# Forget-gate attention: gate bias and causal mask added by VectorE, probabilities turned through HBM by GpSimd's queue

## The chip, the cores and the metric

One core of a Trainium2 chip runs the whole program. The metric is the device time in microseconds of one execution; the kernel before took 1055.29 us (median of 3 runs, 1054.19 to 1055.32).

## What is computed

Two transformer blocks in a row on one sequence of 256 tokens with 1024 channels, all in float32. The change concerns one part of the second block, the attention with a forget gate ("fox"), of 8 heads with 128 channels each:

```python
def fox_attention(q, k, v, f_logit):
    """q,k,v: (B,S,H,dh); f_logit: (B,S,H). logit[t,s] = q.k/sqrt(dh) + sum_{s<j<=t} log f_j, s<=t."""
    c = jnp.cumsum(jax.nn.log_sigmoid(f_logit.astype(jnp.float32)), axis=1).transpose(0, 2, 1)
    ...
        s = jnp.einsum('bqhd,bkhd->bhqk', qi, k32) * scale
        s = s + ci[..., None] - c[:, :, None, :]
        s = jnp.where(kpos[None, :] <= qpos[:, None], s, -jnp.inf)
        p = jax.nn.softmax(s, axis=-1)
        return jnp.einsum('bhqk,bkhd->bqhd', p, v32)
```

The term c of the query is the same for a whole row of scores, so softmax drops it; what is left is a bias by key and the causal mask. The rest of the second block is a gated linear recurrence in chunks ("hgrn2"), a memory attention and two gated feed-forward parts.

## The kernel before

**Weights.** They come as units of 128x2048 floats. SyncE loads them into one of 6 slots (`load`, L591 to L608, two DMAs at L603); for unit u it first waits until TensorE is through with unit u - 6 (L598). ScalarE copies each to a rounded float32r tile `high` (L1368), VectorE subtracts to get the remainder `rest` (L1964), and TensorE multiplies three times, high x high, high x rest and rest x high (`unit`, L820 to L822), 24 matmuls of 512 columns per unit.

**The order of the work.** The projection of the second block, `win2`, has 18 column blocks, thus 36 units. Each engine's program has a loop `for u in range(36)` with a fixed place for every piece of other work: HG_SLOT for the recurrence's levels, FOX_SLOT for the attention: TensorE computes the scores of head n after unit 26 + n and the output of head n - 3 behind them (`fox(n)`, L1173). After the loop comes the block `brA`, in the middle of whose first half stands the last head's output.

**The gates.** In step 7 VectorE cumulates the logarithms of the gates in `fcum`, 40 rows by 256 tokens, where rows 0 to 7 and 32 to 39 hold the same 8 heads (L2522 to L2529). In step 8 ScalarE rounds them to `fbias` (L1742), and VectorE makes rows 32 to 39 the remainder (L2606); the rest of `fbias` is zero (L2531). `fbias` has 384 columns: the 128 keys of the first query tile, then the 256 keys of the second. `fcum` lies in the place into which ScalarE drains the recurrence's inputs in step 9 (`hi_`).

**One head.** `fox(n)` on TensorE: a matmul with a column of `identr`, broadcast, spreads head n's bias over the partitions (L1176, float32r, 384 columns); a matmul of a bf16 identity with `causal` adds the mask on the two diagonal tiles (L1178, 256 columns); two float32 score matmuls add q.k (L1181, recorded as 4). VectorE takes the negated maximum of each query tile (L2553), ScalarE exponentiates with it as the bias and sums (L1814), VectorE scales by the reciprocal of the sum (`fox_scale`, L2081, with L2086 and L2090) and turns the blocks of 32x32 (L2092) into one of 3 slots of `fpT`. SyncE stores that to HBM and reads it back by 4 DMAs in the transposed order of blocks (`turn_probabilities`, L656). These stand behind the weight loads in `load(u)`: the store of head h in unit 32 + h of `win2`, the read one unit later. TensorE multiplies with the values (L1189, L1190), VectorE copies the result out (L2634, L2648).

**GpSimd** runs the differences of the recurrence's decays (`diff`, L751; `cross_diff`, L740), which end near 607 us, and loads gains and small constants by its own queue (L803). After the differences it waits for the last head's output and then loads the memory (L801).

## Time and profile before

| | us |
|---|---|
| median of 3 runs | 1055.29 |
| profiled execution | 1056.9 |
| its span | 1055.1 |
| TensorE busy | 1044.2 (99%) |
| VectorE busy | 755.5 (72%) |
| ScalarE busy | 598.6 (57%) |
| GpSimd busy | 71.0 (7%) |

The profiled execution took 1.8 us more than its span, from the first to the last instruction, and 1.6 us more than the median. Busy times count instructions at work; matmuls are pipelined, so their durations overlap, and the distance between the starts of two is what one costs. TensorE's granted clock is at the full level throughout (0.999 on average).

### The profile page before, as it was taken

Reading aid. Unit: us, or ns where it says so; the run is one execution under the profiler, and the core shown is the slowest. Engines: PE = TensorE matmul, PEld = TensorE weight load, DVE = VectorE, ACT = ScalarE, POOL = GpSimd, SP = SyncE. Lnnn points to the kernel's source line nnn. Section 1 sums busy time; section 2 is a strip of 40 time slices with the busy share of each in tenths; the row PEclk is TensorE's granted clock in tenths of the full one; section 3 lists DMA queues with packets and bytes.
Section 4 is the critical chain, followed back from the end, with each engine's and each line's share of the span. In section 5 each row is a group of like instructions: output and inputs, shape, how many; then the busy total and the mean of one; then the engine's idle time right before and its main releaser. Section 6 shows DMA issues by size and latency. Waiting matters only on the chain.

```text
span 1055.1 us, 12945 instructions
## 1 busy us (share of the span) xinstructions
PE 1044.2 (99%) x4939; PEld 871.8 (83%) x4939; DVE 755.5 (72%) x901; ACT 598.6 (57%) x800; POOL 71.0 (7%) x59
## 2 busy tenths in 40 slices
PE   9999999999999999999999999999999999999997
PEld 7888888878888888888888888888879988888886
DVE  5768777776787676468997778868778666867642
ACT  6473767665384645448774645554366657565531
POOL 1200000000000000000434600000000000000000
PEclk9999999999999999999999999999999999999999
DMA  9945889896487787558857855889875346878751
GB/s 364 390 137 173 293 256 306 272 302 212 177 278 241 246 229 233 188 201 271 250 171 222 240 162 179 266 264 324 298 263 183 120 164 208 236 241 237 246 163 40
DMA packets 97645, 243.89 MB, mean 231 GB/s; under 512 B 15104, under 2 KB 41904, under 8 KB 97456
## 3 DMA queue, kind: packets, MB, share of 16 engines
q1 hardware_dynamic: 94016, 231.51, 67.6%
q0 software_dynamic: 3136, 11.23, 3.1%
q8 instruction: 39, 0.64, 0.2%
q10 hardware_dynamic: 432, 0.33, 0.1%
q14 instruction: 22, 0.18, 0.0%
HBM read 220.48 MB, written 22.54 MB: 230 GB/s over the span
## 4 chain that ended last, share of the span: by engine, by line
PE 76%; DMA 9%; DVE 7%; SPq 3%; issue 2%; ACT 2%; DVEq 0%; ACTq 0%
PE ps L820 17%; PE ps L822 17%; PE ps L821 17%; DMA gv_turned<-gv_blocked 5%; PE ps L857 5%; PE ps L859 5%; PE ps L858 5%; DVE rest L1964 2%; PE ps L954 1%; SPq L641 1%; DMA y_turned<-y_blocked 1%; PE ps L1144 1%; PE ps L1253 1%; PE ps L1255 1%; PE ps L1254 1%
## 5 line engine op out<-in xcount | busy, mean ns | idle before, releaser
L1964 DVE TENSOR_TENSOR rest<-raw,high 128x2048 fp32r<-128x2048 f32 x129 | 295.4, 2306 | 74.7 <-ACT high L1368 74.0
L820 PE MATMUL ps<-high,xt_high 128*128 128x512 f32 x824 | 324.6, 394 | 0.2 <-DVE rest L1964 0.2
L821 PE MATMUL ps<-rest,xt_high 128*128 128x512 f32 x824 | 321.0, 390 | 0.0
L822 PE MATMUL ps<-high,xt_rest 128*128 128x512 f32 x824 | 321.0, 390 | 0.0
L1368 ACT ACTIVATE high<-raw 128x2048 fp32r<-128x2048 f32 x129 | 244.3, 1910 | 68.6 <-DMA raw<-in_units_dram 68.5
L822 PEld LDWEIGHTS ps<-high,xt_rest 128*128 128x128 f32 x824 | 154.7, 188 | 32.3
L820 PEld LDWEIGHTS ps<-high,xt_high 128*128 128x128 f32 x824 | 154.9, 188 | 31.9 <-DVE rest L1964 0.6
L821 PEld LDWEIGHTS ps<-rest,xt_high 128*128 128x128 f32 x824 | 154.9, 188 | 30.9
L1969 DVE SCALAR_TENSOR_TENSOR rest<-raw,wgain,high 128x512 fp32r<-128x512 f32 x176 | 119.1, 746 | 35.7 <-ACT high L1372 35.7
L1372 ACT ACTIVATE high<-raw,wgain 128x512 fp32r<-128x512 f32 x176 | 110.9, 716 | 9.5 <-DMA raw<-in_units_dram 9.5
L1628 ACT ACTIVATE act<-ps,recips 128x256 f32<-128x256 f32 x44 | 18.4, 470 | 85.1 <-PE ps L822 85.0
L821 PE MATMUL ps<-rest,ht_high 128*128 128x512 f32 x168 | 65.4, 389 | 0.0
L822 PE MATMUL ps<-high,ht_rest 128*128 128x512 f32 x168 | 65.4, 389 | 0.0
L820 PE MATMUL ps<-high,ht_high 128*128 128x512 f32 x168 | 65.4, 389 | 0.0
L857 PE MATMUL ps<-high,xt_high 128*128 128x512 f32 x152 | 60.6, 399 | 1.3 <-DVE rest L1964 1.3
L859 PE MATMUL ps<-high,xt_rest 128*128 128x512 f32 x152 | 59.4, 391 | 0.0
L858 PE MATMUL ps<-rest,xt_high 128*128 128x512 f32 x152 | 59.2, 390 | 0.0
L1388 ACT ACTIVATE xt_high<-ps 128x512 fp32r<-128x512 f32 x26 | 15.2, 598 | 58.4 <-PE ps L954 53.0
L2313 DVE SCALAR_TENSOR_TENSOR hid<-ps,recips,act 128x256 f32<-128x256 f32 x44 | 19.2, 478 | 39.7 <-ACT act L1628 39.6
L821 PEld LDWEIGHTS ps<-rest,ht_high 128*128 128x128 f32 x168 | 31.5, 188 | 6.6
L820 PEld LDWEIGHTS ps<-high,ht_high 128*128 128x128 f32 x168 | 31.6, 188 | 6.5
L822 PEld LDWEIGHTS ps<-high,ht_rest 128*128 128x128 f32 x168 | 31.5, 188 | 6.5
(372 smaller groups left out, 1446.0 us busy)
## 6 DMA issues: line engine op xcount, KB each, us to landing
raw<-in_units_dram SPq DMA_DIRECT2D x350, 512.0 KB, 5.0
gv_turned<-gv_blocked SPq DMA_DIRECT2D x11, 512.0 KB, 7.9
gv_t<-gv_turned SPq DMA_DIRECT2D x44, 128.0 KB, 3.1
turned<-blocked SPq DMA_DIRECT2D x22, 256.0 KB, 5.3
hid_t<-turned SPq DMA_DIRECT2D x88, 64.0 KB, 4.1
fox_turned<-fqT SPq DMA_DIRECT2D x6, 512.0 KB, 3.3
raw<-in_units_dram SPq DMA_DIRECT2D x8, 256.0 KB, 4.4
fqT<-fox_turned SPq DMA_DIRECT2D x16, 128.0 KB, 4.2
```

What stands on the lines that cost most here:

```text
L820: pe.matmul(out, sh, wh, start=first, stop=False)
L821: pe.matmul(out, sh, wr, start=False, stop=False)
L822: mm = pe.matmul(out, sr, wh, start=False, stop=last)
L857: pe.matmul(out, sh, wh, start=first, stop=False)
L858: pe.matmul(out, sh, wr, start=False, stop=False)
L859: mm = pe.matmul(out, sr, wh, start=False, stop=last)
L1368: act.activation(high[:, u % SLOTS, c], raw[:, u % SLOTS, c], ACT.Copy).then_inc(unit_high, 1)
L1372: ins = act.activation(high[:, u % SLOTS, c], raw[:, u % SLOTS, c], ACT.Copy, scale=g[:, k:k + 1])
L1628: act.activation(act_[:, j % 2, tt, :], gate_values[:, tt, :], ACT.Silu, scale=recips[:, c:c + 1])\
L1964: vec.tensor_tensor(rest[:, slot, c], raw[:, slot, c], high[:, slot, c].bitcast(F32), ALU.subtract).then_inc(unit_rest, 1)
L1969: ins = vec.scalar_tensor_tensor(rest[:, slot, c], raw[:, slot, c], g[:, q:q + 1], high[:, slot, c].bitcast(F32), ALU.mult, ALU.subtract)
L2313: ins = vec.scalar_tensor_tensor(hid[:, j % 2, :, tt, :], fold(values[:, tt, :]), recips[:, c + tt:c + tt + 1], fold(act_[:, j % 2, tt, :] ...
```

## The change

GpSimd prepares the bias. SyncE stores `fcum` to HBM once (`store_biases`, after the load of unit 13 of `win2`). For each head GpSimd reads the head's row back, spread over the 128 partitions, into one of three float32 tiles (`spread_bias`), and adds `causal` on the two diagonal tiles (`mask_bias`). TensorE computes the score products alone. VectorE's instruction for the maximum becomes one that reads scores and bias, writes -(scores + bias) over the scores in PSUM and keeps the minimum, which is the negated maximum; ScalarE's exponential has the scale -1. Store and reads of the probabilities go from SyncE's queue to GpSimd's. GpSimd's order is: spread 0, spread 1, mask 0, mask 1, then for each head h: spread h + 2, store h, mask h + 2, read h (4 DMAs).

The diff, cut:

```diff
-        fbias = place("fbias", [P, P + S], F32R, area + 62 * KB)
+        fbias = [place(f"fbias{n}", [P, P + S], F32, area + k * KB) for n, k in enumerate((62, 28, 54))]
...
+        fcum_dram = nc.dram_tensor("fcum_rows", (HH, P + S), F32, kind="Internal").ap()
+        def bias_home(h):
+            return fbias[0 if h % 2 == 0 else 1 + h // HALF]
...
-            def turn_probabilities(u):
-
-                h = u - UNIT["win2"] - 33
-                if 0 <= h < HH:
-                    sync.wait_ge(fp_stored, 16 * (h + 1))
-                    src = fp_turned[h].rearrange("(q i) (r e) -> r i q e", q=4, r=4)
-                    for r in range(4):
-                        sync.dma_start(fpT[32 * r:32 * r + 32, h % 3, :].rearrange("p (q e) -> p q e", q=4), src[r]).then_inc(fp_landed[h % 3], 16)
-                h += 1
-                if 0 <= h < HH:
-                    sync.wait_ge(fp_blocked, h + 1)
-                    sync.dma_start(fp_turned[h], fpT[:, h % 3, :]).then_inc(fp_stored, 16)
+            def store_biases(u):
+
+                if u == UNIT["win2"] + 13:
+                    sync.wait_ge(sem("fcum_ready"), 1)
+                    for c0, w in ((0, P), (P, S)):
+                        sync.dma_start(fcum_dram[:, c0:c0 + w], fcum[0:HH, 0:w]).then_inc(fcum_stored, 16)
...
+            def spread_bias(h):
+
+                if h == 1:
+                    pool.wait_ge(aux_done, AUX["lv", 1, 128, 0][0] + 1)
+                elif h == HALF + 1:
+                    pool.wait_ge(aux_done, AUX["fs", HALF - 1][0] + 1)
+                elif h:
+                    pool.wait_ge(sem("fox_max"), TT * (h - 1))
+                pool.dma_start(bias_home(h)[:, :], fcum_dram[h].partition_broadcast(P)).then_inc(fbias_landed[h % 2], 16)
+
+            def mask_bias(h):
+
+                pool.wait_ge(fbias_landed[h % 2], 16 * (h // 2 + 1))
+                d = bias_home(h)[:, :].rearrange("p (n c) -> p n c", n=3)[:, 0:3:2, :]
+                pool.tensor_tensor(d, d, causal[:, :, :], ALU.add).then_inc(fbias_masked, 1)
+
+            def store_probabilities(h):
+
+                pool.wait_ge(fp_blocked, h + 1)
+                pool.dma_start(fp_turned[h], fpT[:, h % 3, :]).then_inc(fp_stored, 16)
+
+            def read_probabilities(h):
+
+                pool.wait_ge(fp_stored, 16 * (h + 1))
+                src = fp_turned[h].rearrange("(q i) (r e) -> r i q e", q=4, r=4)
+                for r in range(4):
+                    pool.dma_start(fpT[32 * r:32 * r + 32, h % 3, :].rearrange("p (q e) -> p q e", q=4), src[r]).then_inc(fp_landed[h % 3], 16)
...
+                    pool.wait_ge(fcum_stored, 32)
+                    pool.wait_ge(consts1_landed, 16 * CONSTS1)
+                    for h in range(2):
+                        spread_bias(h)
+                    for h in range(2):
+                        mask_bias(h)
+                    for h in range(HH):
+                        if h + 2 < HH:
+                            spread_bias(h + 2)
+                        store_probabilities(h)
+                        if h + 2 < HH:
+                            mask_bias(h + 2)
+                        read_probabilities(h)
...
-                    pe.matmul(out[:, 0:P + S], identr[:, n:n + 1].to_broadcast([P, P]), fbias[:, :], start=True, stop=False)
-                    diagonal = out[:, 0:P + S].rearrange("p (n c) -> p n c", n=3)[:, 0:3:2, :]
-                    pe.matmul(diagonal, identb[:, :], causal[:, :, :], start=False, stop=False)
...
-                        mm = pe.matmul(o, fqT[:, n, tt * P:(tt + 1) * P], fox_tokens(fkT, n, *range(tt + 1)), start=False, stop=(tt == TT - 1))
+                        mm = pe.matmul(o, fqT[:, n, tt * P:(tt + 1) * P], fox_tokens(fkT, n, *range(tt + 1)), start=True, stop=True)
...
-                if u == 8:
-                    act.wait_ge(sem("fcum_ready"), 1)
-                    for c0, w in ((0, P), (P, S)):
-                        act.activation(fbias[0:FROWS, c0:c0 + w], fcum[:, 0:w], ACT.Copy).then_inc(sem("fcum_high"), 1)
...
                     elif what == "i":
+                        act.wait_ge(fcum_stored, 32)
                         scaled("win2", j, hi_[:, :, c])
...
-                            ins = act.activation(fp[:, c0:c1], out[:, c0:c1], ACT.Exp,
+                            ins = act.activation(fp[:, c0:c1], out[:, c0:c1], ACT.Exp, scale=-1.0,
...
-                    step(vec.memset(fbias[:, :].bitcast(F32), 0.0))
...
+                        vec.wait_ge(fbias_masked, n + 1)
                         for tt in range(TT):
                             c0, c1 = (0, P) if tt == 0 else (P, P + S)
-                            ins = vec.tensor_reduce(small["negmax"][:, n, tt:tt + 1], src[:, c0:c1], AX_X, ALU.max, negate=True)
-                            ins.then_inc(sem("fox_max"), 1)
+                            vec.tensor_tensor_reduce(src[:, c0:c1], src[:, c0:c1], bias_home(n)[:, c0:c1], -1.0, -3 * NEG,
+                                                     ALU.add, ALU.min, small["negmax"][:, n, tt:tt + 1])\
+                                .then_inc(sem("fox_max"), 1)
...
-                if u == 8:
-                    vec.wait_ge(sem("fcum_high"), 2)
-                    r = slice(FROWS - HH, FROWS)
-                    for c0, w in ((0, P), (P, S)):
-                        vec.tensor_tensor(fbias[r, c0:c0 + w], fcum[r, 0:w], fbias[r, c0:c0 + w].bitcast(F32), ALU.subtract)\
-                            .then_inc(sem("fcum_rest"), 1)
```

Left out above: `identr` and `identb` with the one small instruction and the DMA that fill them, TensorE's waits for them, and a joint semaphore for the stores of other tiles that SyncE turns.

## Rows read from the trace of the kernel before

**Rows 1.** The page, part 1: busy time, share of the span and instructions.

```profile
PE 1044.2 (99%) x4939; PEld 871.8 (83%) x4939; DVE 755.5 (72%) x901; ACT 598.6 (57%) x800; POOL 71.0 (7%) x59
```

**Rows 2.** Busy time by stretch (granted clock, DMA share and GB/s last), heads' stretch.

```profile
634.40:684.00 49.60, 49.40 (x236) 40.16 (x236) 44.01 (x72) 26.06 (x42) 0.00 (x0) 1.00 0.75 234
```

**Rows 3.** Timeline (start, duration) of TensorE at head 0; L1176 of all heads.

```profile
634.68 0.34 PE L1176 MATMUL ps<-fbias,identr 128*128 128x384 f32 x1
...
634.86 0.28 PE L1178 MATMUL ps<-causal,identb 128*128 128x256 bf16 x1
...
634.98 0.82 PE L1181 MATMUL ps<-fkT,fqT 128*128 128x128 f32 x4
...
635.45 0.58 PE L820 MATMUL ps<-high,xt_high 128*128 128x512 f32 x1
...
L1176 PE MATMUL ps<-fbias,identr x8: 337/338/339, 634.7 to 682.3; 128*128 128x384 f32 x8
```

**Rows 4.** Waits from 485 to 600 us: in total, times, longest.

```profile
PE ps L1144 <- DVE hqk L2449: 0.9, 1, 0.9
PE ps L1156 <- DVE hqk L2443: 0.9, 1, 0.9
```

**Rows 5.** Timeline of steps 7 to 10.

```profile
507.26 0.38 DVE L2531 MEMSET fbias<- 128x384 f32 x1
...
518.39 1.27 ACT L1673 ACTIVATE hi<-ps,recips 128x512 f32<-128x512 f32 x2 [3.35 <-PE ps L822]
...
519.55 0.62 DVE L2606 TENSOR_TENSOR fbias<-fcum,fbias 8x128 fp32r<-8x128 f32 x2
...
531.94 1.16 PE L1144 MATMUL ps<-hqk 128*128 128x128 f32 x8 [0.89 <-DVE hqk L2449]
```

**Rows 6.** Tiles fp and fpT: ns min/median/max, first and last start; TensorE's wait.

```profile
L2090 DVE TENSOR_SCALAR fp<-fp,expsum x16: 285/317/349, 640.7 to 689.2; 128x128 f32<-128x128 f32 x8, 128x256 f32<-128x256 f32 x8
...
L2092 DVE STREAM_TRANSPOSE fpT<-fp x8: 577/578/581, 641.3 to 689.6; 128x384 f32<-128x384 f32 x8
...
L1189 PE MATMUL ps<-fpT,fv x16: 377/379/484, 655.0 to 702.4; 128*128 128x256 f32 x16
...
PE ps L1189 <- DMA fpT<-fp_turned: 0.2, 1, 0.2
```

**Rows 7.** DMA issues by line: KB each, median us from issue to landing.

```profile
raw<-in_units_dram SPq DMA_DIRECT2D x350, 512.0 KB, 5.0
...
fp_turned<-fpT SPq DMA_DIRECT2D x8, 192.0 KB, 2.1
fpT<-fp_turned SPq DMA_DIRECT2D x32, 48.0 KB, 3.5
...
gains<-in_gain_mix_pre_dram POOLq DMA_DIRECT2D x1, 512.0 KB, 4.0
gains<-in_gain_hg_norm_dram POOLq DMA_DIRECT2D x1, 512.0 KB, 4.5
...
levelmask<-in_c_levels_dram POOLq DMA_DIRECT2D x1, 143.0 KB, 3.6
```

**Rows 8.** Timeline of GpSimd beside VectorE.

```profile
563.97 2.27 POOL L745 TENSOR_TENSOR crossref<-hb 128x4 f32<-128x4 f32 x1
...
567.34 0.61 POOL L749 TENSOR_TENSOR he_cross<-hb,crossref 128x256 f32<-128x256 f32 x1
...
563.89 2.28 DVE L1964 TENSOR_TENSOR rest<-raw,high 128x2048 fp32r<-128x2048 f32 x1
```

**Rows 9.** Timeline: a head's maxima; last head's product and GpSimd's issues behind it.

```profile
638.41 0.61 DVE L2553 TENSOR_REDUCE negmax<-ps 128x1 f32<-128x128 f32 x2
...
702.57 0.38 PE L1190 MATMUL ps<-fpT,fv 128*128 128x128 f32 x2
...
703.52 0.76 POOL L801 DMA_DIRECT2D mem<-in_mem_dram  x1 [96.08 <-PE ps L1190]
...
704.81 0.53 POOL L803 DMA_DIRECT2D gains<-in_gain_mix_post_dram  x1
```

More of the change, by code:

```diff
@@ L255, in build @@
         for name, shape, dt in (
-            ("ident", [P, P], F32), ("identb", [P, P], BF16), ("causal", [P, TT, P], BF16),
+            ("ident", [P, P], F32), ("causal", [P, TT, P], BF16),
             ("levelmask", [P, MASKS], U8),
@@ L259, in build @@
             ("recips", [P, TT * len(NORMS)], F32), ("moments", [P, TT, 12], F32),
-            ("meanvar", [P, TT, 2], F32), ("identr", [P, HH], F32R), ("eps", [P, 2 + 2 * TT], F32), ("negmax", [P, HH, 2], F32),
+            ("meanvar", [P, TT, 2], F32), ("eps", [P, 2 + 2 * TT], F32), ("negmax", [P, HH, 2], F32),
             ("expsum", [P, HH, 2], F32), ("crossref", [P, TT * HALF], F32), ("lb", [P, 4, HH], F32), ("total", [P, TT * HALF], F32)):
@@ L263, in build @@
             at = -(-marks[name][1] // 32) * 32
-        identr = small["identr"]
         partsum = small["eps"][:, 2:2 + 2 * TT].rearrange("p (a t) -> p a t", a=2)
-        ident, identb, causal = small["ident"], small["identb"], small["causal"]
+        ident, causal = small["ident"], small["causal"]
         levelmask = small["levelmask"]
@@ L402, in build @@
                     nc.dram_tensor("oa_turned", (2, P, D), F32, kind="Internal").ap())
-        mem_turn = (sem("mem_blocked"), [sem(f"mem_stored{n}") for n in range(2)], [sem(f"mem_landed{n}") for n in range(2)],
+        mem_turn = (sem("mem_blocked"), 2 * [sem("mem_stored")], [sem(f"mem_landed{n}") for n in range(2)],
                      nc.dram_tensor("mem_turned", (2, P, D), F32, kind="Internal").ap())
@@ L474, in build @@
         eps_ready = sem("eps_ready")
+        fcum_dram = nc.dram_tensor("fcum_rows", (HH, P + S), F32, kind="Internal").ap()
+        fcum_stored, fbias_masked = sem("fcum_stored"), sem("fbias_masked")
+        fbias_landed = [sem(f"fbias_landed{n}") for n in range(2)]
+        def bias_home(h):
+            return fbias[0 if h % 2 == 0 else 1 + h // HALF]
         fox_blocked, fox_stored = sem("fox_blocked"), sem("fox_stored")
@@ L487, in build @@
         rope_landed = sem("rope_landed")
-        CONSTS1, CONSTS2 = 8, 4
+        CONSTS1, CONSTS2 = 8, 3
         ROOT_ORDER = (("ret", 0),) + tuple((name, tt) for names in (
@@ L607, in load @@
                 turn_tokens(u)
-                turn_probabilities(u)
+                store_biases(u)
             def turn_fox(u):
@@ L641, in turn_conv, with turn @@
                         sync.dma_start(gv_t[32 * r:32 * r + 32, j % 2, :, :], src[r]).then_inc(gv_landed[j % 2], 16)
-            def turn(u, at, sems, n, home, landing=None, turns=1, ready=None, stored_at=None):
+            def turn(u, at, sems, n, home, landing=None, ready=None, stored_at=None):
                 blocked, stored, landed, scratch = sems
@@ L649, in turn @@
                 if u == at + 1:
-                    sync.wait_ge(stored[n], stored_at or 16 * turns)
+                    sync.wait_ge(stored[n], stored_at)
                     src = scratch[n].rearrange("(q i) (r e) -> r i q e", q=4, r=4)
@@ L679, in turn_tokens @@
                 for tt in range(TT):
-                    turn(u, UNIT["brA"] + 9, mem_turn, tt, mem_blocked[:, tt, :])
+                    turn(u, UNIT["brA"] + 9, mem_turn, tt, mem_blocked[:, tt, :], stored_at=16 * TT)
                 for j in range(2):
@@ L683, in turn_tokens @@
                 for j in range(2):
-                    turn(u, UNIT["mk"] + 7 + 2 * j, mem_turn, j, mk_blocked[:, j, :], turns=2, ready=keys_blocked(j))
+                    turn(u, UNIT["mk"] + 7 + 2 * j, mem_turn, j, mk_blocked[:, j, :], ready=keys_blocked(j),
+                         stored_at=16 * (TT + j + 1))
             def turn_hidden(u):
@@ L735, in _ @@
             pool.dma_start(wf_raw[:, :, :], dram["w_flog"].rearrange("p (k n) -> p k n", k=KC)).then_inc(consts2_landed, 16)
-            pool.dma_start(identb[:, :], dram["c_identb"]).then_inc(consts2_landed, 16)
             def clear_scores(hf):
@@ L2333, in _ @@
             ffn("upA", "downA", "ffn1_pre", "win2")
-            vec.tensor_tensor(identr[:, :], ident[:, 0:HH], ident[:, FROWS - HH:FROWS], ALU.add).then_inc(sem("identr_ready"), 1)
             vec.wait_ge(sem("wf_high"), 1)
@@ L2821, in constants @@
     tok = ORDER
-    out = {"c_ident": np.eye(P, dtype=f32), "c_identb": np.eye(P, dtype=f32).astype(np.dtype("bfloat16"))}
+    out = {"c_ident": np.eye(P, dtype=f32)}
     at = tok.reshape(TT, P)
```

3 lines of the change are left out of this document (removed).

## The prediction

> **What bounds the kernel now.** I read the page first: TensorE is busy 99% of the span, the other engines less [rows 1]. So time can only leave by fewer TensorE instructions or by an end to one of the waits in front of them. Next I asked where the heads of the forget-gate attention ("fox") run: in the stretch from 634 to 684 us TensorE is busy 49.4 of 49.6 us and VectorE 44.0 of 49.6, with GpSimd at rest and the DMA engines 75% busy [rows 2]. The reader should see two things there: what is taken from TensorE in this stretch comes off the end one for one as long as nothing makes it wait, and VectorE and the DMA engines have little room for what is moved to them. Only then did I look for waits of TensorE: two of 0.9 us on VectorE in the stages before [rows 4], and one of 0.2 us on a probability that comes back from HBM [rows 6].
>
> **Part 1: two matmuls per head leave TensorE.** Durations on the page overlap (a matmul starts before the last has ended), so the cost is the distance between starts. The bias product (L1176) starts at 634.68, the mask product (L1178) at 634.86, the first score product (L1181) at 634.98: 0.30 us from the first to the third, and there are 8 such heads [rows 3]. The removed work stands wholly on the saturated engine: 8 x 0.30 = **2.4 us**. Bounds: 0.24 us a head if a score product's weight load needs some of the room, 0.30 as read; I take 0.30. The score products become the first of their group, which adds no instruction.
>
> **Part 2: preparation of the bias.** VectorE loses one memset (0.38 us) and two subtractions (0.62 us together), at 507 and at 520 us [rows 5], and ScalarE two copies. Between 507 and 531 us VectorE has practically no pause, and at 531 us TensorE waits 0.9 us for its decays [rows 4, 5]. So 1.0 us of VectorE work leaves a chain that ends in that wait, from which between 0 (another input of the chain was as late) and 0.9 can be had; the two waits follow each other on the same chain, so 0.9 is the most for both together. Nearer the upper end, since the work is on VectorE itself: **0.6 us**. Added: SyncE, after loading unit 13 of the block, waits for the cumulated gates and stores them by two small DMAs. They are complete when that memset starts, at 507.3 us [rows 5]. That load itself can be issued only when TensorE is through unit 7 (line 598), whose logits the gates come from, so SyncE waits for little; what is queued behind it are weight loads five units ahead of their use. ScalarE now waits for that store before it drains the inputs at 518.4 us [rows 5]. With the 2.1 us of the nearest store [rows 7] it is there by about 512. Cost 0; if the cover of some 6 us were gone, ScalarE would be late with weights that TensorE uses units later.
>
> **Part 3: addition while the maximum is taken.** Two reductions per head take 0.61 us together [rows 9]; the new instruction reads a second operand and writes PSUM. No row shows it. Below: the same 0.61, since it walks as many elements; above: twice, 1.2. I take 0.75, so 8 x 0.15 = 1.2 us more on VectorE. That lies beside TensorE: in step u VectorE prepares the weights of unit u + 4 (line 2547). Cost 0 on the path, but it uses up room: 44.0 + 1.2 in a stretch that becomes 49.6 - 2.4 = 47.2 us long. VectorE also waits for GpSimd's mask; behind it stand the scaling of the last head and the next weights.
>
> **Part 4: GpSimd masks the bias.** Eight additions of 128x256. The nearest row takes 0.61 us; but an addition of 4 columns took 2.27 us, from 563.97 to 566.24, in which VectorE's two-input subtraction ran from 563.89 to 566.17 [rows 8]. So one of these engines waited for the other to finish, and a mask costs 0.6 to 2.9 us on GpSimd, or up to 0.6 on VectorE. I take 0.6 and keep 8 x 0.6 = 4.8 us as VectorE's upper bound. The Trainium skill ("SBUF — State Buffer", practical consequences of the shared ports) says that a VectorE instruction with two SBUF inputs contends with a GpSimd instruction that reads SBUF, and that the loser blocks fully; the row agrees, 2.27 us against 2.28.
>
> **Part 5: the way of the probabilities.** This decides. A head's blocked probabilities are ready at 641.9 (641.3 + 0.58) for the first and 690.2 for the last, so every 48.3 / 7 = 6.9 us; TensorE wants them at 655.0 and 702.4 [rows 6]. That is 13.1 and 12.2 us later. After the change the heads follow every 6.6 us and the room is about 12.2 to 12.5. SyncE loses 8 stores and 32 reads, and the waits in front of its weight loads; the 0.2 us wait of TensorE for a probability [rows 6] ends with them: **0.2 us** (0 to 0.2). GpSimd gets 8 spreads of the bias, 8 stores and 32 reads, at 0.53 us an issue [rows 9]. It takes up to 0.57 us from the releasing matmul's end (702.95) to GpSimd's issue (703.52) [rows 9]; bounds 0 and 0.57, I take 0.3 for each wait. A store of this size lands after 2.1 us from SyncE's queue, a read after 3.5 [rows 7]. From GpSimd's queue the nearest rows are reads: 3.6 us for 143 KB, 4.0 and 4.5 for 512 KB, against 5.0 for a weight load of 512 KB from SyncE. So the queue adds little; bounds for the store 2.1 and 4.5, taken 2.6 (nearest to the row of the same store); for the 192 KB bias 2.8 and 4.5, taken 3.6; for a read 4.0. The Trainium skill ("DMA: Bandwidth & Descriptors", anatomy of one DMA) gives about 2.0 us plus bytes over 436 GB/s for a DMA of this path; by it, as an estimate, store and spread would both take 2.5 us, and no wait would arise anywhere.
>
> One head then: 0.3 + 2.6 to the landed store, 0.3 more, four issues of 0.53 (2.1), last read begun at +4.8 and landed at +8.8, against 12.2: 3.4 us over. But GpSimd's queue is served in order, so the round counts too. By the store: 0.53 + 0.3 + 2.6 + 0.3 + 2.1 = 5.8 us. By the bias: 3.6 to land, 0.3 + 0.6 for the mask, 0.3 + 2.1 for the reads behind it = 6.9 us. Against 6.6 that falls behind by 0.3 a head, over five rounds 1.5 us, less than the 3.4 at hand. Each mask is finished in the round two heads before VectorE uses it. So the cost is 0, with a thin cover.
>
> **Sum.** 2.4 + 0.6 + 0.2 = 3.2 us off. The profiled execution took 1056.9 us (span 1055.1), so 1053.7 for its like; it stands 1.6 us over the median of the runs, 1055.29, so I forecast a median of **1052.1**. Of its own, with parts between 2.0 and 3.5 and scatter, this case spans 1051.0 to 1053.3.
>
> **Rivals.**
> (a) *The bias round becomes the bound.* If the spread lands after 4.5 us (as the 512 KB row), a round is 7.8 us, five of them fall behind by 6.0, and TensorE waits 2.6 us for head 5's probabilities. For it: DMA engines 75% busy, masks that may wait up to 2.3 us. Against: 192 KB only. It begins at a landing of 4.0 us. Time: 1052.1 + 2.6 = 1054.7, no change by my bound. VectorE getting slower by 4.8 us of contention ends about here too.
> (b) *Slower: the serial queue of GpSimd.* If also the store takes 4.5 us from this queue, each round is 3.2 + 4.5 = 7.7 us, and the last head lands 7 x 7.7 + 0.3 + 4.5 + 0.3 + 1.6 + 4.0 = 64.6 us after the first was blocked. TensorE wants it after 60.5 - 6 x 0.3 = 58.7. Stall 5.9 us, net +2.7: 1058.0, slower by 0.26%. In general the end is at 28.6 + 8 x store time: it decides from 3.8 us on, and at 4.2 the gain is gone. For it: no software-queue row is under 3.6 us. Against: those are reads, and a store here lands much sooner than a read (2.1 against 3.5).
> (c) *Issues that wait for VectorE.* Scaling the probabilities takes VectorE two instructions of about 0.3 us a head [rows 6]. If one issue per round waited for both, 0.6 x 5 = 3.0 us more backlog to the 1.5 gives a stall of 1.1: 1053.2. The rows give little for it: the issues that are shown take the same 0.53 us [rows 9]. The Trainium skill ("SBUF — State Buffer", the trap in which VectorE blocks a DMA) has this rule: while VectorE runs a two-port operation, GpSimd can't write its descriptors.
> (d) *Less is removed than it looks*: the wait at 531 us stays, as another input was as late: 1052.7.
>
> **How the numbers follow.** A measurement of this kernel can tell about 0.2%, 2.1 us, from no change: faster is below 1053.2, slower above 1057.4. Chances: forecast 0.46, (a) 0.22, (b) 0.15, (c) 0.08, (d) 0.09. Faster: forecast and (d), and half of (c), less scatter around the bound: 0.55. Slower: (b) and a worst (a): 0.17. The rest, 0.28, is no change. The range goes from 1050.9 (0.3 less if the VectorE chain gives all of its 0.9, and 0.9 of scatter, as the runs shown differ by 1.1) to 1056.6; it takes in the forecast, (a), (c), (d) and the milder end of (b), and leaves out about 2 in 10.
>
> **What would show it.** The first score product of a head follows the last weight product 0.30 us sooner; TensorE's wait at 531 us is shorter or gone; no TensorE wait on the probabilities' DMA. The store from GpSimd's queue lands under 3.8 us and the spread under 4.0. A head's last read is issued about 5 us after its block and not more than 7 by head 5. I am wrong if TensorE waits for these reads by over 1 us in all, if the stores land as late as reads, or if VectorE's mask waits delay its weights.

## The result, and the profile after

| | before | after |
|---|---|---|
| median of the runs compared | 1055.29 us (5 runs, 1054.19 to 1055.55) | 1067.02 us (5 runs, 1064.81 to 1069.99) |
| ratio, 95% interval | 1 | 1.0113 (1.01 to 1.0126) |
| profiled execution: time, span | 1056.9, 1055.1 | 1067.02, 1065.0 |

The changed kernel is slower by 1.1%, about 12 us: outside the range, on the other side from the forecast. The page, part 1, of the changed kernel:

```profile
PE 1044.0 (98%) x4923; PEld 871.0 (82%) x4923; DVE 755.8 (71%) x913; ACT 598.4 (56%) x798; POOL 106.7 (10%) x114
```

Beside [rows 1] this one line splits the loss. The span grew by 9.9 us, and TensorE's busy time fell by 0.2. So its idle time went from 10.9 us (1055.1 - 1044.2) to 21.0 (1065.0 - 1044.0). Sixteen matmuls are gone, yet their time did not leave the busy time: something made the others slower by as much. Both are found below.

The waits of the changed kernel (who waits, for what: us in total, times, longest):

```profile
POOL fbias L801 <- DMA fbias<-fcum_rows: 23.6, 7, 6.2
...
POOL fpT L813 <- DMA fp_turned<-fpT: 13.0, 4, 4.5
PE ps L1228 <- DMA fpT<-fp_turned: 11.4, 5, 7.5
...
DVE ps L2585 <- POOL fbias L801: 6.1, 3, 3.0
...
PE ps L1186 <- DVE hqk L2481: 0.3, 1, 0.3
```

The third line is the loss: TensorE waits 11.4 us for probabilities, where [rows 6] had 0.2. The first two show GpSimd waiting 36.6 us for its own transfers. In the last, the wait at 531 us is 0.3 instead of 0.9 [rows 4].

DMA issues of the changed kernel (KB each, median us to landing), to be read against [rows 7]:

```profile
fbias<-fcum_rows POOLq DMA_DIRECT2D x8, 192.0 KB, 4.6
fp_turned<-fpT POOLq DMA_DIRECT2D x8, 192.0 KB, 4.7
fpT<-fp_turned POOLq DMA_DIRECT2D x32, 48.0 KB, 4.2
```

The store takes 4.7 us where SyncE's took 2.1; one by one they took 4.6, 4.1, 7.3, 7.8, 5.4, 3.5, 4.8 and 4.4. GpSimd's timeline of the changed kernel shows what that does to a queue served in order (start, duration, and in brackets the idle time before):

```profile
655.03 0.57 POOL L795 DMA_DIRECT2D fbias<-fcum_rows  x1
655.60 0.56 POOL L806 DMA_DIRECT2D fp_turned<-fpT  x1
662.31 2.77 POOL L801 TENSOR_TENSOR fbias<-fbias,causal 128x256 f32<-128x256 f32 x1 [6.15 <-DMA fbias<-fcum_rows]
665.03 2.20 POOL L813 DMA_DIRECT2D fpT<-fp_turned  x4
667.22 0.57 POOL L795 DMA_DIRECT2D fbias<-fcum_rows  x1
667.79 0.56 POOL L806 DMA_DIRECT2D fp_turned<-fpT  x1
673.21 0.67 POOL L801 TENSOR_TENSOR fbias<-fbias,causal 128x256 f32<-128x256 f32 x1 [4.86 <-DMA fbias<-fcum_rows]
675.92 2.19 POOL L813 DMA_DIRECT2D fpT<-fp_turned  x4 [2.04 <-DMA fp_turned<-fpT]
```

Read it from spread to spread: 655.03 to 667.22 is one round of 12.2 us (the stores, 655.60 and 667.79, are as far apart). It is the whole chain laid end to end: 7.28 until the mask starts, right after the spread has landed, 2.72 until the reads start behind the mask, 2.19 for their four issues. The next round ends with the store at 678.67, after 10.9 us; there the store was the last to land. Over all eight, the stores go from 640.50 to 700.37, one round every 59.9 / 7 = 8.6 us (7.9, 7.2, 12.2, 10.9, 8.5, 5.9 and 7.3), where a head comes every 6.6. GpSimd waits for a head's probabilities only before the first store (2.3 us), so VectorE's waits for masks do not lengthen the round.

TensorE's timeline of the changed kernel, first two heads and the longest wait:

```profile
632.93 0.81 PE L1220 MATMUL ps<-fkT,fqT 128*128 128x128 f32 x4
...
639.05 0.82 PE L1220 MATMUL ps<-fkT,fqT 128*128 128x128 f32 x4
...
683.45 1.22 PE L1228 MATMUL ps<-fpT,fv 128*128 128x256 f32 x2 [7.55 <-DMA fpT<-fp_turned]
684.46 0.63 PE L1229 MATMUL ps<-fpT,fv 128*128 128x128 f32 x2
684.75 0.77 PE L862 MATMUL ps<-high,xt_high 128*128 128x512 f32 x1
685.32 0.63 PE L863 MATMUL ps<-rest,xt_high 128*128 128x512 f32 x1
685.75 0.63 PE L864 MATMUL ps<-high,xt_rest 128*128 128x512 f32 x1
...
687.22 0.39 PE L862 MATMUL ps<-high,xt_high 128*128 128x512 f32 x1
687.45 0.40 PE L863 MATMUL ps<-rest,xt_high 128*128 128x512 f32 x1
```

The row of the kernel before that answers to the first two is the second head's bias product:

```profile
641.13 0.34 PE L1176 MATMUL ps<-fbias,identr 128*128 128x384 f32 x1
```

While nothing waits, the first two heads start 6.12 us apart (639.05 - 632.93), before 6.45 (641.13 less the 634.68 of [rows 3]). After the wait of 7.55 us the matmuls start 0.43 us apart (685.75 - 685.32) until 687, then again 0.23. That is the other part of the loss: the granted clock. By stretch (busy time of PE, PEld, DVE, ACT, POOL; then granted clock, DMA share, GB/s):

```profile
634.40:684.00 49.60, 39.17 (x179) 31.84 (x178) 40.30 (x75) 21.58 (x37) 20.32 (x31) 0.96 0.78 246
684.00:703.00 19.00, 19.00 (x83) 15.79 (x82) 14.35 (x26) 9.13 (x13) 9.86 (x18) 0.92 0.55 169
```

Before, the first stretch had TensorE busy for 49.40 us at clock 1.00 [rows 2]. In the second stretch it is busy throughout and still loses: a mean clock of 0.92 over 19 us is 1.5 us of work. The page hides this: 8 x 0.33 = 2.6 us of matmuls left, the busy time fell by 0.2 only, so 2.4 came back. The clock explains 1.5 of them by this stretch, and some more by the matmuls just ahead of it; the exact share is not shown.

The groups of the new instructions in the changed kernel (ns min/median/max, first and last start):

```profile
L2585 DVE CUSTOM_DVE_ANT_0 ps<-ps,fbias x16: 292/380/467, 636.7 to 692.4; 128x128 f32<-128x128 f32 x8, 128x256 f32<-128x256 f32 x8
...
L801 POOL TENSOR_TENSOR fbias<-fbias,causal x8: 664/672/2772, 623.1 to 690.2; 128x256 f32<-128x256 f32 x8
```

### The profile page after: what moved, and what is told of

It is laid out like the page before. It is cut to its first block, busy times and chain, and to the rows that moved or that the text cites. A ratio compares the mean times of both kernels' runs of the same rounds, so it can differ in the third digit from the quotient of the medians.

```text
span 1065.0 us, 12950 instructions
## 1 busy us (share of the span) xinstructions
PE 1044.0 (98%) x4923; PEld 871.0 (82%) x4923; DVE 755.8 (71%) x913; ACT 598.4 (56%) x798; POOL 106.7 (10%) x114
## 4 chain that ended last, share of the span: by engine, by line
PE 80%; DMA 8%; DVE 5%; POOL 2%; issue 2%; ACT 1%; SPq 1%; DVEq 0%; ACTq 0%
PE ps L862 18%; PE ps L864 18%; PE ps L863 18%; PE ps L899 5%; PE ps L901 5%; PE ps L900 5%; DMA fp_turned<-fpT 2%; DMA fbias<-fcum_rows 2%; DVE rest L1997 2%; POOL fpT L813 2%; DMA y_turned<-y_blocked 1%; PE ps L996 1%; DMA mem_turned<-mem_blocked 1%; SPq L661 1%; PE ps L1186 1%
```

## The experiments

All times are medians, each beside runs of the kernel before on the same chip; the chip changed between groups of runs, so two variants are best compared by their ratios (95% intervals in brackets). Line numbers of variants differ by some tens.

| run | what it is | median us (runs) | ratio to before |
|---|---|---|---|
| e1_probs_sync | bias by GpSimd, probabilities by SyncE | 1057.46 (11) | 1.0023 (1.0013 to 1.0032) |
| e2_only_probs_pool | before, probabilities by GpSimd | 1058.76 (6) | 1.0041 (1.0025 to 1.0057) |
| e3_reads_first | after, reads ahead of the mask | 1069.13 (4) | 1.0125 (1.011 to 1.014) |
| e4_no_bias_matmuls | before without the two matmuls | 1053.60 (11) | 0.9987 (0.9979 to 0.9996) |
| e5_reads_ahead | e1, reads ahead of weights | 1070.45 (4) | 1.0146 (1.0124 to 1.0168) |
| e6_two_spreads | e1, two spreads in all | 1056.78 (11) | 1.001 (1.0001 to 1.002) |
| e7_spreads_by_scalar | after, spreads issued by ScalarE | 1063.59 (5) | 1.0086 (1.0073 to 1.01) |
| e8_hardware_queues | e5, spreads issued by ScalarE | 1074.08 (4) | 1.0183 (1.0169 to 1.0197) |
| e9_probs_pool_gated | e2, with SyncE's two waits kept | 1060.56 (6) | 1.0053 (1.0038 to 1.0067) |
| e10_tokens_last | e1, token tile behind the probabilities | 1055.53 (12) | 1.0011 (1.0 to 1.0022) |
| e11_after_gated | after, with SyncE's two waits kept | 1065.77 (4) | 1.0104 (1.009 to 1.0119) |
| e12_before_tokens_last | before, token tile behind the probabilities | 1054.57 (11) | 1.0003 (0.9994 to 1.0011) |
| e13_loads_held | e9, weights wait for the store's landing | 1058.79 (1) | before 1055.43 (1) |

### Which half costs: e1, e2 and e4

e1 gives the probabilities back to SyncE (`turn_probabilities` as before) and leaves the bias with GpSimd:

```diff
+                turn_probabilities(u)
                 store_biases(u)
...
-                    for h in range(HH):
-                        if h + 2 < HH:
-                            spread_bias(h + 2)
-                        store_probabilities(h)
-                        if h + 2 < HH:
-                            mask_bias(h + 2)
-                        read_probabilities(h)
+                    for h in range(2, HH):
+                        spread_bias(h)
+                        mask_bias(h)
```

> The changed kernel, with the stores and reads of the probabilities back on SyncE's queue where they stood before; spreads and masks stay with GpSimd. If the in-order queue of GpSimd, which serves both ways in one round of 8.6 us (640.5 to 700.4 in 7 rounds), is the cause: all of the loss goes and the gain shows, 1055.3 - 2.4 (matmuls) - 0.6 (VectorE's chain) = about 1052.3, no wait of TensorE for probabilities above 0.3 us. If the masks that VectorE waits for are the cause (6.1 us in three waits): the waits of 1 to 3 us stay and the time is above 1056. If the two matmuls were worth nothing: about 1055.3 and no waits.

e2 is the kernel before with only the move of the queue:

```diff
-                turn_probabilities(u)
...
+                    for h in range(HH):
+                        store_probabilities(h)
+                        read_probabilities(h)
```

> The kernel before with one part of the change alone: stores and reads of the probabilities by GpSimd's queue; bias and mask stay matmuls. Queue theory: a round is a store that lands after 4.7 to 5.2 us and four issues of 0.55, thus 7.2 to 7.7 us against heads every 6.9; behind by 0.3 to 0.8 a head, and with 0.3 + 5 + 0.3 + 1.7 + 4.2 = 11.5 us of a head's own way against 12.2 to 13.1 of room: TensorE waits 1 to 5 us, time 1056 to 1060. If only both ways in one queue make the loss: no wait, 1055.1. If the software queue's landing alone makes all of it: 1065 or more.

e4 takes the two matmuls out of the kernel before and puts nothing in their place:

```diff
-                    pe.matmul(out[:, 0:P + S], identr[:, n:n + 1].to_broadcast([P, P]), fbias[:, :], start=True, stop=False)
-                    diagonal = out[:, 0:P + S].rearrange("p (n c) -> p n c", n=3)[:, 0:3:2, :]
-                    pe.matmul(diagonal, identb[:, :], causal[:, :, :], start=False, stop=False)
```

> The kernel before without the two matmuls per head that add bias and causal mask; scores go unmasked and without bias to the softmax, all else stays. Prices the removal alone: 8 x 0.30 = 2.4 us, 1052.9, if the distance between starts is what they cost. Rival: the probabilities' way (0.2 us of wait already) takes back up to 1 us, as its room shrinks by 0.6 to 0.9 us: 1053.3 to 1053.9. If TensorE's time were hidden in another stage: 1055.3.

Each half alone loses: 0.23% of 1055 is 2.4 us for the bias half, 0.41% is 4.3 us for the queue half. Together they lose 11.9 (1.13%), some 5 us more than the sum of 6.7. So the two halves hurt each other. e7 below, which takes the spreads out of the queue that they share, gives back more than half of these 5 us.

In e2 the stores follow each other every (692.17 - 641.51) / 7 = 7.2 us, with no bias between them, and that alone makes TensorE wait 2.1 us in two. DMA issues of e2's sibling e9 are below; its own stores landed after 4.7 us (median). So the store is slow from GpSimd's queue without any spread beside it.

e4 shows what the removal is worth when nothing is added: 0.13% or 1.4 us, not 2.4. TensorE's waits of e4:

```profile
PE ps L1186 <- DMA fpT<-fp_turned: 1.2, 2, 0.6
```

The wait for probabilities was 0.2 us [rows 6] and is 1.2 here, with the old queue and the old instructions. A faster TensorE asks for them sooner, and their way does not get shorter: of 2.4 us, 1.0 turns into a new wait. That holds for every version that leaves the probabilities' way as it is; e4 does not contain the shorter preparation of part 2, which is worth up to 0.9 us more.

e1 is the same, with the spreads added to the traffic. SyncE's timeline of e1:

```profile
658.02 0.95 SPq L610 DMA_DIRECT2D raw<-in_units_dram  x2
659.01 2.35 SPq L662 DMA_DIRECT2D hg<-oa_turned  x4
661.41 1.95 SPq L671 DMA_DIRECT2D fpT<-fp_turned  x4
```

The stretches of e1 (columns as above), from 650 us on:

```profile
650.00:660.00 10.00, 10.00 (x49) 8.39 (x48) 9.85 (x20) 2.72 (x5) 3.83 (x4) 1.00 0.77 253
660.00:670.00 10.00, 7.61 (x36) 5.80 (x34) 9.05 (x18) 6.37 (x11) 1.22 (x2) 1.00 1.05 277
670.00:680.00 10.00, 9.88 (x40) 8.14 (x41) 7.86 (x13) 4.61 (x8) 1.18 (x2) 0.83 0.88 285
```

Head 2's four reads stand in SyncE's queue behind 1 MB of weights and the four reads of a token tile, in a stretch where the DMA engines are saturated (1.05). The last of them landed after 7.15 us; TensorE waited 2.4 us for it, until 670.12, and then ran its matmuls 0.43 us apart until 674.7 (clock 0.83). The wait and the slower stretch behind it are more than the gain.

### Order in GpSimd's queue: e3 and e7

e3 reads a head's probabilities before it masks:

```diff
                         store_probabilities(h)
+                        read_probabilities(h)
                         if h + 2 < HH:
                             mask_bias(h + 2)
-                        read_probabilities(h)
```

> The changed kernel with one line moved: GpSimd reads head h back before it masks head h + 2. Queue theory: a read no longer waits for the spread's landing (7.2, 5.9 and 5.5 us in the middle heads) and the mask; the round is 0.57 + store landing of about 5 + 2.2 + 0.7 = 8.5 or somewhat less than before, since the mask's wait is hidden behind the store: 1058 to 1064, 3 to 9 us under the changed kernel. If spread and mask did not matter: unchanged at 1067. Masks should not come later than VectorE asks for them by more than 1 us.

A miss: 1069.13, the changed kernel's time or worse (the profiled execution, 1074.16, is the longest of its four). The round is 8.85 us (stores from 641.56 to 703.48), TensorE waits 10.9 us in three. With the mask out of the reads' way the store alone holds them up for 35.0 us in eight waits, so taking the mask away gains nothing: the store is as slow as the spread (medians 4.3 and 4.1 us). VectorE's waits for a mask grow from 6.1 to 12.1 us, up to 4.4 each, where the expectation allowed 1. The useful line is the last store of e3's timeline, when the block's weights are nearly all loaded:

```profile
701.31 2.18 POOL L813 DMA_DIRECT2D fpT<-fp_turned  x4 [3.21 <-DMA fp_turned<-fpT]
703.48 0.56 POOL L806 DMA_DIRECT2D fp_turned<-fpT  x1
705.92 2.18 POOL L813 DMA_DIRECT2D fpT<-fp_turned  x4 [1.88 <-DMA fp_turned<-fpT]
```

The stretch between them (columns as above):

```profile
704.04:706.50 2.46, 2.46 (x8) 1.87 (x7) 2.46 (x2) 2.13 (x2) 0.58 (x3) 0.50 0.27 100
```

The store lands after 2.2 us and the reads begin after 2.4, at a DMA share of 0.27 behind the issue. GpSimd's queue can store in the time that SyncE's takes [rows 7].

e7 moves the spreads of the changed kernel to ScalarE's queue, behind its wait for the maxima (and the first two to step 25):

```diff
+                        if n + 2 < HH:
+                            act.dma_start(bias_home(n + 2)[:, :], fcum_dram[n + 2].partition_broadcast(P)).then_inc(sem(f"bias_landed{n % 2}"), 16)
...
-                        if h + 2 < HH:
-                            spread_bias(h + 2)
```

> The changed kernel with the spreads issued by ScalarE, behind its wait for a head's maximum; masks, stores and reads of the probabilities stay with GpSimd. If the coupling of the two ways in GpSimd's queue (a store is issued right behind a spread and lands no sooner: 7.3 and 7.8 us behind spreads of 7.2 and 5.9) makes the difference between e2 (1058.8) and the changed kernel (1067): 1056 to 1059. If the probabilities' own way by the software queue is all that counts: 1065 or more.

1063.59: 3.4 us back by the medians, 2.8 by the ratios, whose intervals just touch. TensorE's wait for probabilities falls from 11.4 to 5.8 us, and the round from 8.6 to (694.99 - 644.04) / 7 = 7.3. The spreads still land after 5.2 us and the stores after 4.4; seven of the eight reads now wait for the store, 21.1 us in all. So a part of the loss is the spread's place in GpSimd's round. The larger part stays, with a round about as long as e2's.

### The traffic of the spreads: e6

```diff
-                    for h in range(2, HH):
-                        spread_bias(h)
-                        mask_bias(h)
...
-                        vec.wait_ge(fbias_masked, n + 1)
+                        vec.wait_ge(fbias_masked, min(n + 1, 2))
```

> Run e1_probs_sync with only the first two biases spread and masked; heads 2 to 7 add one of these two again in place of their own. It takes 6 spreads of 192 KB and 6 masks away. If the spreads crowd the DMA engines from 650 to 670 us: TensorE's wait falls to about 1 us, as in e4_no_bias_matmuls (1.2 us), time 1053.6. If GpSimd's traffic is innocent and only TensorE's earlier arrival makes the wait: 1057 as e1.

Beside e1, 0.7 us less (0.13%, and the intervals overlap). Wait for probabilities 1.6 us instead of 2.4, and no stretch at the lower clock in the profiled execution. So the 1.2 MB of spreads are at most a small part of e1's loss, and nearer to the second branch of the expectation than to the first; even without them this form is not shown to be faster than before.

### The same round on SyncE's queue: e5 and e8

e5 is e1 with the reads issued ahead of the unit's weights, the store behind them, so that the reads overtake the traffic that e1 showed; the store now follows the weights without a wait between them:

```diff
             def load(u):
 
+                read_turned(u)
...
-                turn_probabilities(u)
+                store_turned(u)
```

> Run e1_probs_sync (probabilities by SyncE, bias by GpSimd) with each read of the probabilities put ahead of the unit's weight load and of the other tile's reads in SyncE's queue instead of behind them. Transport theory: e1 is slower than before because head 2's reads are issued at 661.4 to 663.4, behind 1 MB of weights and 512 KB of another tile while the DMA engines are at 100%, land after 7.2 us and stop TensorE for 2.4 us, after which its granted clock falls for some 4 us. Ahead of these they are issued at about 660 and land in 3 to 5 us: no wait over 0.5 us, clock 1.00 throughout, 1052.3. Rival, that VectorE's additional work or the masks delay the probabilities: waits stay, 1057.

e8 is e5 with the spreads issued by ScalarE as in e7.

> Run e5_reads_ahead with the spreads issued by ScalarE; GpSimd only masks, and no DMA of this stage goes by its queue. Transport theory: the spreads land in 3 to 4 us instead of 3.3 to 6.6, nothing else changes, since no wait hangs on them: equal to e5 within 0.5 us, 1052.0 to 1052.8. If ScalarE's issues delay its exponentials and weights: above e5 by 1 us or more.

Both miss by far: 1070.45 and 1074.08. That e8 lies above e5 is the second branch of its expectation; the cause of that difference was not looked for. A wait and the landings of e5:

```profile
SPq L672 <- DMA fp_turned<-fpT: 38.2, 8, 6.6
```

```profile
fp_turned<-fpT SPq DMA_DIRECT2D x8, 192.0 KB, 5.2
fpT<-fp_turned SPq DMA_DIRECT2D x32, 48.0 KB, 2.0
```

The reads do land sooner (2.0 us instead of e1's 3.7). But the store now stands directly behind 1 MB of weights and lands after 5.2 (3.5 in e1), and SyncE waits 38.2 us for the eight stores, with all weights queued behind that wait. This is the changed kernel's fault made again on the other queue: a store behind loads lands late, and a queue that waits for it in order passes the delay on. No software queue takes part in the stores here.

### What made the store slow: e9, e11 and e13

In the kernel before, SyncE waits for the probabilities, stores them, and only then issues the next weights. The change took that wait away from the weights too. e9 is e2, and e11 the changed kernel, with SyncE's two waits back and nothing moved by them:

```diff
+            def turn_probabilities(u):
+                h = u - UNIT["win2"] - 33
+                if 0 <= h < HH:
+                    sync.wait_ge(fp_stored, 16 * (h + 1))
+                h += 1
+                if 0 <= h < HH:
+                    sync.wait_ge(fp_blocked, h + 1)
```

> Run e2_only_probs_pool (before, with stores and reads of the probabilities by GpSimd) with SyncE's two waits per head kept: its weight loads stand behind the same events as before, though it moves nothing for the heads. Theory of collisions: the store landed after 2.0 us for five of eight heads before because SyncE's wait held the next 1 MB of weights back until the store was issued; in e2 weights are under way when it starts (landing 3.1 to 7.0). With the waits kept the store from GpSimd's queue lands after about 3 us (2.2 us was seen in idle stretches), TensorE's waits for probabilities fall from 2.1 to under 0.5 us, time 1055 to 1056.5. If the software queue itself is slow: landings stay at 4.7, time 1058 or more.

> The changed kernel with SyncE's two waits per head kept as in e9. If collisions with weight loads are the larger part of its loss: 1057 to 1061. If the serial round of GpSimd's queue with spread, mask, store and reads is (8.6 us against heads every 6.6): 1064 or more, as holding the weights back only shortens the store's landing.

Neither helps clearly: 1060.56 against e2's 1058.76, 1065.77 against 1067.02 for the changed kernel, with intervals that overlap in both pairs. The landings of e9:

```profile
fp_turned<-fpT POOLq DMA_DIRECT2D x8, 192.0 KB, 4.9
fpT<-fp_turned POOLq DMA_DIRECT2D x32, 48.0 KB, 4.4
```

Store and weights are now released by the same event, in two queues, and the DMA engines are 73 to 101% busy in the 2 us from each store's issue. To wait for the same thing is not to stand ahead in the queue: SyncE's weights go out at 641.70, 655.82 and 665.96 us, the stores of these heads at 641.97, 657.62 and 668.40, the later ones behind the last head's reads. It left two theories: the loads beside it slow the store, or GpSimd's queue does. e13 holds the weights until the store has landed:

```diff
-                    sync.wait_ge(fp_blocked, h + 1)
+                    sync.wait_ge(fp_stored, 16 * (h + 1))
```

> The kernel of e9 (only the probabilities by GpSimd's queue) with one change: SyncE holds the next weight units of each head until the head's store has landed, where in e9 it held them only until the probabilities lay ready, and the stores still landed after 4.9 us (median). The theory that the loads of weights, issued in the same moment, slow the store: the eight stores now land in 2.2 to 3 us, as the one store of e3 did that met no load (2.2). The rival, that a store from GpSimd's queue takes over 4 us whatever runs beside it: they still land in 4.5 to 5 us. In both cases the weights start later by the landing, so that TensorE may come to wait for them; the time may be anything from 1056 to 1070 and decides nothing.

The stretches of e13 from the end of each store's issue to its reads (length, busy times, clock, DMA share, GB/s), first six heads:

```profile
641.94:643.79 1.85, 1.85 (x9) 1.50 (x8) 1.85 (x4) 0.17 (x1) 0.00 (x0) 1.00 0.26 106
649.31:651.17 1.86, 1.86 (x10) 1.50 (x8) 1.86 (x4) 0.00 (x0) 0.00 (x1) 1.00 0.26 106
655.99:658.92 2.93, 2.93 (x14) 2.43 (x13) 2.93 (x5) 0.00 (x0) 0.00 (x1) 1.00 0.55 219
663.31:667.93 4.62, 4.62 (x24) 3.75 (x23) 4.55 (x9) 2.18 (x5) 0.00 (x1) 1.00 0.76 179
670.66:677.03 6.37, 5.63 (x29) 4.35 (x27) 3.94 (x11) 4.14 (x7) 0.00 (x0) 1.00 0.68 225
679.76:685.35 5.59, 4.79 (x24) 3.66 (x24) 3.57 (x7) 2.62 (x5) 0.01 (x2) 1.00 0.83 256
```

From the start of each store's issue to its landing, the measure of all landings here, it is 2.1, 2.1, 3.2, 4.9, 6.7 and 5.9 us (the last two 4.2 and 3.8); a stretch and 0.6 us of issue are 0.3 more, since the reads start that much behind the landing. The expectation of 2.2 to 3 for all eight fails: held weights are only later weights, and from the fourth head on they run when the next store is issued. But the order is plain: 2.1 us twice at a DMA share of 0.26, 3.2 at 0.55, 3.8 and more wherever it is 0.65 or more (the last two as well, 0.65 and 0.66). The closest pair is that of the first two stores: in e9, with weights beside them, they landed after 5.7 and 4.8 us, in e13, with the weights held, after 2.1 both. The rival, over 4 us whatever runs beside it, is out. The changed kernel fits: its one store at a share under 0.8 in its first 2 to 3 us (687.16 us, 0.57) landed after 3.5 us, the others (0.87 to 1.04) after 4.1 to 7.8. The share does not fix the time, though: e2's sixth store landed after 3.1 us at 0.73, e9's third after 8.3 at 0.76.

SyncE's stores in the kernel before landed, one by one, after 1.8, 1.9, 2.0, 4.6, 2.0, 6.5, 2.1 and 4.3 us. The stretches from the third and the fourth store of the kernel before:

```profile
657.33:659.33 2.00, 2.00 (x11) 1.65 (x10) 2.00 (x5) 0.00 (x0) 0.00 (x0) 1.00 0.84 185
663.28:665.28 2.00, 2.00 (x11) 1.63 (x10) 1.59 (x1) 0.38 (x1) 0.00 (x0) 1.00 1.17 224
```

The third landed in 2.0 us though the share was 0.84: the 512 KB store ahead of it in its queue landed by 657.4, and the weights were issued behind it, at 657.80. When the fourth was issued, half of a unit's weights and a token tile's reads were still in flight ahead of it; it took 4.6. So the load slows a store on either queue, and SyncE's place ahead of the weights had sheltered five of its eight. Not shown is whether GpSimd's queue is also slower than SyncE's under the same load; in quiet stretches 2.1 to 2.2 us stand against 1.8 to 2.0.

### Order on SyncE's queue: e10 and e12

e10 is e1 with the token tile's DMAs behind the probabilities' in a unit; e12 does that to the kernel before, as a control:

```diff
-                turn_tokens(u)
                 turn_probabilities(u)
+                turn_tokens(u)
```

> Run e1_probs_sync with the other tile's turn (oa, 512 KB each way) put behind the probabilities' store and reads in SyncE's program instead of ahead. Head 2's reads are then issued at about 659 instead of 661.4, behind 1 MB of weights only. Transport theory: TensorE's wait of 2.4 us for head 2 and the fall of its clock go, 1052.5 to 1054. If the order against this tile doesn't matter: 1057. If the other tile is now late, TensorE waits in front of brA.

> Control for e10: the kernel before with that order of SyncE's program. It had one wait of 0.2 us for probabilities, so 1054.9 to 1055.3. If it is faster than that by more than 0.5 us, e10's gain is the order's and not a removed wait's; if it is slower, the other tile's delay costs something.

e10 lies 1.9 us under e1 by the medians (1055.53), 1.3 by the ratios (1.0011 against 1.0023), with intervals that overlap; the forecast of 1052.5 to 1054 is missed, and the control moves nothing (1.0003). TensorE's wait in e10:

```profile
PE ps L1238 <- DMA fpT<-fp_turned: 2.0, 2, 1.4
```

Two waits of at most 1.4 us took the place of one of 2.4, and the clock stays at 1.00 in every stretch of 10 us. This is the fastest complete version of the change that was run, about level with the kernel before, not ahead of it.

## Why the prediction was wrong

**Part 1, the matmuls: right.** The heads' scores start 6.12 us apart instead of 6.45, 0.33 a head against the 0.30 taken. Missing was what e4 measured: 1.0 us of the 2.4 becomes a longer wait for the probabilities, even with nothing moved. The text subtracted the 0.2 us wait, when it was the first sign of the next bound.

**Part 2, the preparation: right in size, less firm than told.** The wait at 531 us is 0.3 instead of 0.9 us in the changed kernel, as predicted; in e1 it is 0.7, in e3 0.8. No wait on SyncE's store of the gates (508 us) shows in the profile.

**Part 3, the maximum: right.** The new instruction, twice with its read of the result (0.29, 0.14, 0.47 and 0.14 us, overlapping), takes 0.73 us from the first start to the last end (636.66 to 637.39); 0.75 was taken. VectorE's waits of 6.1 us for a mask come from GpSimd's round and not from here.

**Part 4, the mask: right.** 0.67 us in the median, 2.77 when VectorE's two-operand subtraction runs beside it: so both bounds of the text occurred. The subtraction ran from 662.26 to 664.55, the mask from 662.31 to 665.08. The Trainium skill's rule ("SBUF — State Buffer", practical consequences of the shared ports) is borne out a second time.

**Part 5, the way of the probabilities: this step failed,** by its landing times. Taken were 2.6 us for the store, 3.6 for the spread and 4.0 for a read; measured 4.7, 4.6 and 4.2. The store's 2.1 us was read as a price of the transfer. It was the price in one place: for five of eight heads SyncE stored when its last loads had landed and the next ones stood behind the store in its own queue. Moved to another queue, the same 192 KB run beside 512 KB loads. What e13, e3 and e5 show in its place is a landing time that goes with the load that the store meets: from GpSimd's queue 2.1 to 2.2 us in quiet stretches (shares of 0.26 and 0.27 behind the issue) and 3.1 to 8.3 under load, from SyncE's 2 us ahead of the weights and 5.2 behind them. By the Trainium skill ("DMA: Bandwidth & Descriptors", anatomy of one DMA) the estimate for this size is 2.5 us; the runs come near it only in the quiet stretches.

The round follows. It was put at 6.9 us by the bias and is 8.6 in the mean, 12.2 at worst. The chain of its members was right and sums to that worst round; the sizes were wrong, and the single values hid that a late spread (7.2 us) and a slow mask (2.77) can fall together. Against 6.6 us a head, six of the seven rounds add to the backlog and one (5.9) works a little off; what ends it is that TensorE waits.

**The rivals.** What happened is (a) and (b) in one round. In six rounds both a spread and a store are in flight: in four of them the reads follow the mask at once, so the spread held them up, as in (a), and in two they wait for the store, as in (b) [GpSimd's timeline above has one of each]. (b) had a chance of 0.15, and (a) was priced at no change. With the measured 4.7 us, (b)'s formula gives 28.6 + 8 x 4.7 = 66.2 against 58.7, a stall of 7.5 us, and for the profiled execution 1053.7 + 7.5 = 1061.2. To 1067.0 it lacks 5.8; the waits are 11.4 - 7.5 = 3.9 longer and up to 2.4 went to slower matmuls, 0.5 more than is missing. That it comes this near is in part luck: for e2, the store alone in the queue, the same formula gives 66.2 - 60.5 = 5.7 us of stall, and TensorE waited 2.1.

(c) happened too, once, at the last head. The text had read one duration for all issues, 0.53 us, though [rows 9] also has one of 0.76. GpSimd's issues take 0.54 to 0.59 us in this stretch, but the last head's four reads took 3.64 us instead of 2.2, while VectorE scaled the gate, not the probabilities:

```profile
705.04 3.64 POOL L813 DMA_DIRECT2D fpT<-fp_turned  x4 [4.11 <-DMA fp_turned<-fpT]
...
706.20 2.36 DVE L2674 TENSOR_SCALAR gate<-gate 128x2048 f32<-128x2048 f32 x2
```

Two of the four issues, at 706.12 and 707.53, took 1.41 and 1.15 us. TensorE waited 0.77 us for this head's reads (711.73), so at most that much of the 11.4 is (c)'s. (d) was small and is unsettled, with 0.3 to 0.8 us left of the wait.

**The cover.** 3.4 us of room were set against a round that already lost 0.3 us a head by its own estimate, with ends of 2.1 and 4.5 for the store. A difference of two near numbers, multiplied by five rounds, deserved a far wider range, and more than 0.15 on the side where its sign turns (from 3.8 us on).

**Left open.** How the DMA engines share between queues in detail, whether GpSimd's queue is slower than SyncE's under the same load, and why exactly a 48 KB read takes what it takes, was not tried. A version in which GpSimd's order waits on nothing (spreads all done before the first head) was not run: three bias tiles are too few for it.

## What to carry to other kernels

The time from issue to landing belongs to a place in the schedule, not to a transfer: before a DMA is moved, look at each of its landings one by one, at the DMA share beside it, and at what the issuing queue held back on its behalf. A queue that waits for its own transfers has a round, the sum of its landings and issues, and the round has to be shorter than the period of the work with a margin for the slow ones. And when time is taken off the bounding engine, a small wait behind the shortened stretch can be the next bound (0.2 us became 1.2 in e4): price it as growing, not as going away.

## What was not expected of the hardware

- A long wait of TensorE was paid for twice here. After a wait of 7.55 us the changed kernel's matmuls started 0.43 us apart for some 3 us instead of 0.23; after a wait of 2.39 us e1's did so for 3.4 us (671.3 to 674.7). The granted clock falls to 0.50 in such a stretch (e9, 665 to 670 us), the 1.2 GHz level instead of the 2.4. e7 and e11, with waits of 3.3 us, show such stretches too (0.57 from 671 to 675 us, 0.50 from 682 to 686). In e6, e10 and e13, whose longest waits for probabilities were 1.6, 1.4 and 1.4 us, no stretch shows it, nor does the changed kernel after its waits of 1.3 and 1.6 us.
- The same store of 192 KB took from 1.8 us (SyncE, kernel before) to 7.8 (GpSimd, changed kernel; 8.3 in e9), and within the kernel before alone from 1.8 to 6.5.
- Two queues released by one event do not keep the order of a single queue: e9's stores took 4.9 us (median) with the same waits in front of the weights, where SyncE's own queue gave 2.1. The weights went out 0.3 to 2.4 us ahead of the stores.
